# A two-layer encoder trunk: loops written out on five engines, waits turned into constants

## What is computed

```
for l in range(DEPTH):
    ada = (silu(c) @ w_ada[l] + b_ada[l]).reshape(B, 9, D)      # modulation: shift, scale, gate x 3
    u = modulate(rmsnorm(x, norm_g[l, 0]), ada[:, 0], ada[:, 1])
    x = x + 0.5 * ada[:, 2] * swiglu(u, w_ff1_up[l], w_ff1_down[l])
    u = modulate(rmsnorm(x, norm_g[l, 1]), ada[:, 3], ada[:, 4])
    x = x + ada[:, 5] * token_mixing(u)          # window attention and pooling, gated, then w_out
    u = modulate(rmsnorm(x, norm_g[l, 2]), ada[:, 6], ada[:, 7])
    x = x + 0.5 * ada[:, 8] * swiglu(u, w_ff2_up[l], w_ff2_down[l])
```

## Time and profile before

| what | value |
|---|---|
| median of three runs | 2163.26 us |
| lowest and highest of them | 2158.65 and 2165.34 us |
| span of the profiled execution | 2167.4 us |
| instructions in it | 30219 |
| PE busy | 2103.8 us |
| mean granted clock of PE | 0.978 |

### The profile page before, as it was taken

One profiled execution on the slowest core, in us unless ns is written; L12 is line 12 of the kernel. 1 busy time (PEld: TensorE's weight loads), 2 busy tenths in 40 slices (PEclk: granted clock), 3 DMA queues, 4 the chain that ended last, 5 costly groups with the idle time before them and its releaser, 6 DMA issues.

```text
span 2167.4 us, 30219 instructions
## 1 busy us (share of the span) xinstructions
PE 2103.8 (97%) x10214; PEld 1775.1 (82%) x10214; DVE 987.4 (46%) x1609; ACT 571.0 (26%) x850; POOL 955.2 (44%) x471
## 2 busy tenths in 40 slices
PE   7999999998999999999999999999989999999999
PEld 7888888886887888878888888888868788888887
DVE  5733234268658643223345422335856766332332
ACT  1322222231422422222222222222233224123222
POOL 0644344345245554334445533444443456443443
PEclk6999999999999999999999999999999999999999
DMA  7344345332345355254425524442423544432333
GB/s 272 108 136 140 91 146 163 71 117 83 93 127 183 88 162 161 68 146 137 136 59 172 155 75 145 137 134 67 141 69 112 156 151 126 131 100 79 98 100 104
DMA packets 343634, 267.49 MB, mean 123 GB/s; under 512 B 27094, under 2 KB 306990, under 8 KB 343470
## 3 DMA queue, kind: packets, MB, share of 16 engines
q1 hardware_dynamic: 341792, 264.80, 40.8%
q10 hardware_dynamic: 1678, 0.55, 0.1%
HBM read 263.21 MB, written 2.10 MB: 122 GB/s over the span
## 4 chain that ended last, share of the span: by engine, by line
PE 79%; issue 12%; POOL 5%; DVE 2%; DMA 1%; ACTq 0%; DVEq 0%; POOLq 0%; ACT 0%; SPq 0%
PE bank L1214 23%; PE bank L1215 22%; PE bank L1216 22%; POOL w_lo L561 5%; PE bank L1277 1%; PE bank L1278 1%; PE bank L1281 1%; PE ps L1485 1%; PE ps L1299 1%; POOL pool_s L575 1%; PE ps L1237 1%; PE ps L1236 1%; PE ps L1235 1%; PE bank L1235 1%; PE bank L1237 1%
## 5 line engine op out<-in xcount | busy, mean ns | idle before, releaser
L561 POOL TENSOR_TENSOR w_lo<-stage,w_hi 128x1024 fp32r<-128x1024 f32 (+2 forms) x342 | 856.8, 2519 | 1107.2 <-ACT w_hi L619 1060.2
L1214 PE MATMUL bank<-u_hi,w_hi 128*128 128x512 f32 x1792 | 713.2, 398 | 10.5 <-issue 7.5
L1215 PE MATMUL bank<-u_lo,w_hi 128*128 128x512 f32 x1792 | 701.4, 391 | 0.0
L1216 PE MATMUL bank<-u_hi,w_lo 128*128 128x512 f32 x1792 | 701.3, 391 | 0.0
L619 ACT ACTIVATE w_hi<-stage 128x1024 fp32r<-128x1024 f32 (+2 forms) x340 | 353.5, 1071 | 207.2 <-DMA stage<-in_w_pool_o 66.3
L1214 PEld LDWEIGHTS bank<-u_hi,w_hi 128*128 128x128 f32 x1792 | 339.2, 189 | 82.9 <-issue 11.8
L1216 PEld LDWEIGHTS bank<-u_hi,w_lo 128*128 128x128 f32 x1792 | 338.9, 189 | 72.0
L1215 PEld LDWEIGHTS bank<-u_lo,w_hi 128*128 128x128 f32 x1792 | 339.4, 189 | 70.9 <-issue 2.9
L1214 PE MATMUL bank<-h_hi,w_hi 128*128 128x512 f32 x744 | 292.1, 393 | 6.1 <-POOL w_lo L561 6.1
L909 DVE TENSOR_TENSOR prod<-silu,bank 128x512 f32<-128x512 f32 x88 | 60.5, 687 | 515.9 <-PE bank L1216 493.1
L889 DVE SCALAR_TENSOR_TENSOR ada_acc<-ada_stage,c_act,ada_acc 128x512 f32<-128x512 f32 x252 | 268.0, 1064 | 52.5 <-DMA ada_stage<-in_w_ada 47.9
(11 more groups left out here) (160 smaller groups left out, 1680.6 us busy)
## 6 DMA issues: line engine op xcount, KB each, us to landing
stage<-in_w_ff_up SPq DMA_DIRECT2D x176, 512.0 KB
ada_stage<-in_w_ada SPq DMA_DIRECT2D x256, 256.0 KB, 3.5
stage<-in_w_ff_down SPq DMA_DIRECT2D x32, 1408.0 KB
stage<-in_w_in SPq DMA_DIRECT2D x18, 1024.0 KB
stage<-in_w_out SPq DMA_DIRECT2D x10, 1024.0 KB
ada_first<-in_w_ada SPq DMA_DIRECT2D x16, 512.0 KB, 12.2
stage<-in_w_in SPq DMA_DIRECT2D x16, 256.0 KB
stage<-in_w_in SPq DMA_DIRECT2D x8, 512.0 KB
```

Of the source, the lines that this page charges most:

```text
L561: nc.gpsimd.tensor_tensor(stage_tile(w_lo, kind, n), t, hi_tile(n, depth(kind, n)), ALU.subtract).then_inc(lo_ready, 1)
L1214: mm(bank[n % BANKS][:, :], hi[:, k, :], rhs_hi(k), start=(k == 0), stop=False)
L1215: mm(bank[n % BANKS][:, :], hi[:, k, :], rhs_lo(k), start=False, stop=False)
L1216: last = mm(bank[n % BANKS][:, :], lo[:, k, :], rhs_hi(k), start=False, stop=(k == k_n - 1))
```

## The change

- The layer loop and the loops over the halves are written out in Python on all five engines, so that each layer and each half has code of its own, and l and half are numbers. The addresses of loads and the values that waits compare with become constants. The branches around PE's first three tiles and around SP's modulation loads go.
- `ff_pieces` gives how many modulation pieces a half has: 24, but in the last layer's second block 16 in half 0 and none in half 1. SP, DVE and PE use it.
- The gates of a feed-forward block are computed once, in half 0, instead of in both halves.
- Rounding (ACT) and low parts (POOL) for tiles past the last one go, and with them SP's two last loads of `w_out` and the wait for them.

The core of the diff (the same edits of loops stand for all engines):

```diff
+        def ff_pieces(l, i, half):
+
+            return FF_ADA if l < DEPTH - 1 or i == 0 else 2 * KT * (1 - half)
...
-                                         up_v[l, :, :, bass.ds((half * HALF_FT + n) * P + j * D_FF, P)]
+                                         up_v[l, :, :, (half * HALF_FT + n) * P + j * D_FF:(half * HALF_FT + n + 1) * P + j * D_FF]
...
-                    while sent < FF_ADA and FF_STEPS[max(sent - 2, 0)] + 4 <= 2 * n:
+                    while sent < ff_pieces(l, i, half) and FF_STEPS[max(sent - 2, 0)] + 4 <= 2 * n:
...
-                if g < 2:
-                    with sp.If(half < 1):
-                        sp.wait_ge(ada_used, free)
-                        sp.dma_start(ada_stage[a % 2][:, :], src[l, k, :, first + g * ADA_W:first + (g + 1) * ADA_W]
-                                     ).then_inc(ada_in[a % 2], 16)
-                    with sp.Else():
-                        next_layer(slice((g + 1) * ADA_W, (g + 2) * ADA_W))
-                else:
-                    next_layer(bass.ds(half * 3 * ADA_W, ADA_W))
+                own = half == 0 and g < 2
+                at = first + g * ADA_W if own else (half * 3 + g - 2) * ADA_W
+                sp.wait_ge(ada_used, free)
+                sp.dma_start(ada_stage[a % 2][:, :], src[l if own else l + 1, k, :, at:at + ADA_W]
+                             ).then_inc(ada_in[a % 2], 16)
...
-            with sp.Fori(0, DEPTH) as l:
-                with sp.Fori(0, 2) as half:
+            for l in range(DEPTH):
+                for half in range(2):
                     ff_half(l, 0, half, w_ff1_up, w_ff1_down)
...
-            for s in range(2):
-                sp.wait_ge(tile_done, DEPTH * TILES + 2 * s - 5 + DONE)
-                sp.dma_start(stage[s][:, 0:KT * 2 * P].rearrange("p (k c) -> p k c", c=2 * P),
-                             w_out.rearrange("l (k p) n -> l p k n", p=P)[0, :, :, 0:2 * P]).then_inc(loaded[s], LOADED)
...
-                    for n in range(FF_TILES):
+                for half in range(2):
+                    for n in range(FF_TILES - AHEAD * (l == DEPTH - 1 and half == 1)):
                         low_part("ff", tiles_before(l, 2, half), n + AHEAD)
...
-                    round_weights("ff", tiles, loads, n + AHEAD)
+                    if tiles + n + AHEAD < DEPTH * TILES:
+                        round_weights("ff", tiles, loads, n + AHEAD)
...
-                    if n and n % 8 == 0 and n // 8 <= FF_GROUPS:
+                    if n and n % 8 == 0 and n // 8 <= ff_pieces(l, i, half) // KT:
                         ada_group(l, i, half, n // 8 - 1)
-                    if n == 18:
+                    if n == 18 and half == 0:
                         make_gate(l, i, half)
-                    if n < FF_ADA:
+                    if n < ff_pieces(l, i, half):
                         ada_piece(l, i, half, n)
...
-                    if n and n % 8 == 0 and n // 8 <= FF_GROUPS:
+                    if n and n % 8 == 0 and n // 8 <= ff_pieces(l, i, half) // KT:
                         ada_reduce(l, i, half, n // 8 - 1)
...
-                with pe.If(half > 0):
+                if half > 0:
                     for n in range(FIRST):
                         one(n)
...
-            with pe.Fori(0, DEPTH) as l:
+            for l in range(DEPTH):
                 norm(l, 0, "ff")
-                with pe.Fori(0, 2) as half:
+                for half in range(2):
                     ff_half(l, 0, half)
```

More of the change, by code:

```diff
@@ L435, in ff_half @@
                         m = 2 * (n - HALF_FT)
-                        sp.dma_start(dst[:, :, :], down_v[l, :, bass.ds(half * HALF_FT, HALF_FT), m * P:(m + 2) * P]
+                        sp.dma_start(dst[:, :, :], down_v[l, :, half * HALF_FT:(half + 1) * HALF_FT, m * P:(m + 2) * P]
                                      ).then_inc(loaded[s], LOADED)
-                    while sent < FF_ADA and FF_STEPS[max(sent - 2, 0)] + 4 <= 2 * n:
+                    while sent < ff_pieces(l, i, half) and FF_STEPS[max(sent - 2, 0)] + 4 <= 2 * n:
                         ada_piece(l, i, half, sent)
                         sent += 1
-                assert sent == FF_ADA
+                assert sent == ff_pieces(l, i, half)
             def ada_piece(l, i, half, a):
@@ L452, in ada_piece @@
                     sp.wait_ge(ada_used, free)
-                    sp.dma_start(ada_stage[a % 2][:, :], src[l, k, :, bass.ds(first + g * ADA_W + half * 3 * ADA_W, ADA_W)]
+                    sp.dma_start(ada_stage[a % 2][:, :], src[l, k, :, first + (g + half * 3) * ADA_W:first + (g + half * 3 + 1) * ADA_W]
                                  ).then_inc(ada_in[a % 2], 16)
                     return
-                def next_layer(column):
-                    with sp.If(l < DEPTH - 1):
-                        sp.wait_ge(ada_used, free)
-                        sp.dma_start(ada_stage[a % 2][:, :], src[DEPTH - 1, k, :, column]).then_inc(ada_in[a % 2], 16)
-                    with sp.Else():
-                        sp.wait_ge(ada_used, free)
-                        sp.sem_inc(ada_in[a % 2], 16)
-                if g < 2:
-                    with sp.If(half < 1):
-                        sp.wait_ge(ada_used, free)
-                        sp.dma_start(ada_stage[a % 2][:, :], src[l, k, :, first + g * ADA_W:first + (g + 1) * ADA_W]
-                                     ).then_inc(ada_in[a % 2], 16)
-                    with sp.Else():
-                        next_layer(slice((g + 1) * ADA_W, (g + 2) * ADA_W))
-                else:
-                    next_layer(bass.ds(half * 3 * ADA_W, ADA_W))
+                own = half == 0 and g < 2
[3 more added lines that the diff above has]
+                             ).then_inc(ada_in[a % 2], 16)
             def mix(l):
@@ L548, in _ @@
             sp.wait_ge(stored, 16 * 2 * JT)
-            for s in range(2):
-                sp.wait_ge(loaded[s], LOADED * (DEPTH * LOADS // STAGE_SLOTS + 1))
         @block.gpsimd
@@ L589, in _ @@
                 low_part("ff", 0, n)
-            with pool.Fori(0, DEPTH) as l:
+            for l in range(DEPTH):
                 u_low(l, 0)
-                with pool.Fori(0, 2) as half:
+                for half in range(2):
                     for n in range(FF_TILES):
@@ L733, in _ @@
                 nc.scalar.activation(hi_tile(n, KT), stage_tile(stage, "ff", n), ACT.Copy).then_inc(hi_ready, 1)
-            with act.Fori(0, DEPTH) as l:
+            for l in range(DEPTH):
                 round_u(l, 0)
-                with act.Fori(0, 2) as half:
+                for half in range(2):
                     ff_half(l, 0, half)
@@ L792, in make_gate @@
                 at = 3 * i * KT
-                count = 10 * l + (0, 4, 6)[i] + 2 * half
+                count = 6 * l + 2 * i
                 dve.wait_ge(ada_added, groups_before(l, i) + 3)
@@ L895, in ada_group @@
                 dve.wait_ge(ada_reduced, count + 2)
-                s = ada_sum[:, bass.ds(3 * i * KT + 4 * g + half * 12, 4)]
+                at = 3 * i * KT + 4 * g + half * 12
+                s = ada_sum[:, at:at + 4]
                 nc.vector.tensor_tensor(s, s, ps7[:, 0:4], ALU.add).then_inc(ada_added, 1)
@@ L1176, in _ @@
             nc.vector.tensor_copy(ada_sum[:, (N_ADA - 2) * KT:], ps7[:, 0:2 * KT]).then_inc(ada_added, 1)
-            with dve.Fori(0, DEPTH) as l:
+            for l in range(DEPTH):
                 nc.vector.tensor_copy(lay[:, :], vec[:, l, :]).then_inc(vec_step, 1)
@@ L1182, in _ @@
                 normalise(l, 0)
-                with dve.Fori(0, 2) as half:
+                for half in range(2):
                     ff_half(l, 0, half)
```

1 line of the change is left out of this document (removed).

## The result

The changed kernel takes 2141.69 us, median of 4 runs (2135.38 to 2146.22), against 2162.82 us of the kernel before (4 runs) on the same chip: ratio 0.9901, 95% interval 0.9879 to 0.9924. That is 1.0% less; 2141 was predicted. Its profiled execution spans 2144.4 us (forecast 2145.7). Later runs of it gave 2140.77 us, ratio 0.9892 (0.9875 to 0.9909).

What follows compares the result with a forecast made beforehand. PE, busy 97% of the span, bounds the kernel. 8.9 + 4.3 + 2.9 + 3.6 + 2.0 = 21.7 us off takes the span from 2167.4 to 2145.7 and the median from 2163.26 to 2141.6; predicted 2141, range 2128 to 2155.

Steps and rivals of the forecast that it cites:

- Half turns: PE's branch back at four half turns: 8.9 us of idle time goes, plus 4.3 us of low clock behind.
- The stretch at half clock: Behind two of the four half turns PE runs at clock 0.50; 1.00 expected after all four, 4.3 us, bounds 0 and 4.3.
- Layer turn: Start of layer 1: DVE's 2.92 us under "issue" goes, worth 2.9 us; PE's own branch lies under it.
- Groups: Last feed-forward block: four groups of modulation products on PE go, 0.90 us each, 3.6 us.
- Loads past the end: Two w_out transfers, three ACT roundings and three POOL subtractions behind the last tiles go, worth 0.
- SyncE's register operations: Operations ahead of SyncE's transfers go, shortening PE's waits for POOL's low parts and a modulation sum: 2.0 us, bounds -2 and 12.
- The high bound: For SyncE's register operations, 12 us: the stalls and a low clock behind them vanish.
- Another wait in the branch's place: Rival at the half turns: another wait, such as rounding L619, keeps 13.2 us and 8.5 go: 2155, 10%.
- the first row's releaser (the rounding): First half turn's idle row names ACT rounding L619; sign for the rival of another wait; the three other rows name nothing.
- Long rows that only tell of a full queue: Rival: long branch rows show only a sequencer held up behind queued products; removal gains nothing there: 2157.7, 4%.
- Straight-line code late: Rival: each written-out half is new code that arrives late; twelve arrivals exposed on PE, 35 us, give 2177; 4%.
- Pool step: Rival in token mixing: PE's two 6.0 us waits counted unchanged; may vanish (2128) or grow by half (2147); 12%.

Runs made afterwards that it cites:

- PE's half loops alone: Kernel before with only PE's loops over the halves written out, layer loop and other engines' loops kept: 2146.57 us, ratio 0.9927.
- the kernels of the table: Kernel before (2162.82 us), changed kernel (2141.69) and four between: PE's half loops written out, all PE, four engines with SyncE's loops kept, all modulation pieces kept.
- the control: The changed kernel run once more with nothing edited: 2140.77 us.
- the one with SyncE slowed: Changed kernel with five long-met register waits on SyncE ahead of every weight transfer in the two token mixings: 2142.69 us, ratio 0.9901.

## Why the prediction was right, step by step

- **Half turns, 8.9 + 4.3 = 13.2; measured 14.5 in the stages, 14.6 in the medians of PE's half loops alone.** The mechanism is shown: PE's branch back, a step in price with distance, on PE alone. The size was 1.3 us short, 0.2 to 0.4 a turn: 5.83, 3.85, 2.52 and 2.34 against 2.65 + 2.9, 2.01 + 1.4, 2.15 and 2.12. Where it went is seen when the starts of PE's products behind each turn are set against those of the changed kernel. Before the first turn's idle time and behind it stand

  ```profile
  243.99 0.28 PE L1237 MATMUL bank<-h_hi,w_lo 128*128 128x256 f32 x1
  ...
  247.48 0.63 PE L1215 MATMUL bank<-u_lo,w_hi 128*128 128x512 f32 x1
  ```

  The first product starts 246.92 - 243.99 = 2.93 us behind the last one, 0.12 in the changed kernel: 2.8 us lost where the brackets say 2.65, because the next product would have started 0.16 us before the last one's end. At the four turns this makes 9.6 instead of 8.9 us. The first product is itself longer (0.77 and 0.47 us in the earlier trace rows), which puts the second start off by another 0.3, 0.1, 0.1 and 0.1 us, 0.6 together. The stretch at half clock lost 4.2 us (4.3 forecast), and 0.2 us went just ahead of the turns. So the term was short by the two small parts, and the clock came as forecast. Why the clock fell behind turns 1 and 2 and not behind 3 and 4, with 2.0 to 2.7 us of idle time ahead of each, no run here shows.

  The Trainium skill, "Runtime: NRT & Kernel Launch", section Instruction fetch mechanics, gives PE a store of 2048 instructions; that lies between the 1600 that were cheap and the 2200 that were not, but the half loop with its 1803 records paid too, so the price begins somewhat below that figure here. The Trainium skill's 108 ns for a compare-and-branch ("Advanced Engine Details and Errata", section Control Flow Timing) fit neither the 0.076 of a branch that falls through nor the 0.208 and 3.4 to 3.6 us of one that turns back.
- **Layer turn, 2.9; measured 2.96.** That PE's own branch counts nothing there was shown by writing out PE alone; that DVE is the engine that counts is argued from its row.
- **Groups, 3.6; measured 3.6.** Loads past the end at 0: nothing in the last stages speaks against it.
- **SyncE's register operations, 2.0 (-2 to 12): open.** Taking them away gave 0.1 us in the medians (2143.55 to 2143.43), putting a like delay back 1.9; both are inside what these runs can tell. The mixings were 2.3 us shorter in the profile, but 4.1 us lie between two profiles of one program. The high bound is out: PE's waits for the low parts did not vanish, they move between 4.6 and 10.1 us among the kernels of the table, the control and the one with SyncE slowed. The three other parts, 14.5, 2.96 and 3.6 us, already make the 21.1 us between the medians and leave nothing for this one. The sum is within 1 us of the median because one term was 1.3 us too small and this one seems to be 2 too large; that nearness is luck.
- **Rivals.** Another wait in the branch's place: no, the first row's releaser (the rounding) meant nothing once the branch was gone. Long rows that only tell of a full queue: no, 14.6 us came with their removal. Straight-line code late: no, not one "issue" in PE's list, and fewer packets of code. Pool step: its 12.0 us stayed to a tenth of a microsecond in every one of these kernels with DVE's old order, so the overlap didn't slide as I thought it might. The prediction called it DVE late while POOL runs; 7.6 us of it were the order of DVE's own work, and 4.4 are open.

## What to carry to other kernels

A loop on the bounding engine costs by how far back its branch goes: here 0.2 us up to 1600 instructions, wholly hidden when a short loop turned once, and 3.4 to 4.2 us from some 1800 on, of which 2.3 to 5.8 us a turn reached the time, low clock included. Write out the loops whose body is longer than that, on the engine that the end waits for; on the others only where PE waits for their first result. And when a list of waits shows two equal waits that no edit moves, read the order of work on the releasing engine: moving one short step forward there gave 9.6 us, nearly half of what the whole change gave.

## What the runs showed of the hardware that was not expected

The step in the branch's price between 1600 and 2200 instructions. A short branch that turns back takes 0.208 us on PE, not the 0.05 to 0.07 of DVE. Two waits written one after another went into one instruction, 0.106 us from start to start. And the two token mixings vary by up to 10 us together between executions of nearly the same code, with the granted clock at 0.97 to 0.99 over each stage, while the feed-forward halves repeat to 0.3 us.
